# A two-layer GLA and Gated DeltaNet trunk on one core: another order at the program's beginning, a gate product of two matmuls, and stores of the chunk systems in ten pieces

## The reference

```python
def rms_norm(x, w):
    y = xf * lax.rsqrt(jnp.mean(xf * xf, axis=-1, keepdims=True) + NORM_EPS)
    return (y * w.astype(jnp.float32)).astype(x.dtype)

def gdn_mixer(h, w_in, conv_w, a_log, dt_bias, head_norm, w_out):
    proj = h @ w_in
    qkv, z, beta_logit, a_logit = jnp.split(proj, [...], axis=-1)
    ...
    beta = jax.nn.sigmoid(beta_logit.astype(f32))
    log_a = -jnp.exp(a_log.astype(f32)) * jax.nn.softplus(a_logit.astype(f32) + dt_bias.astype(f32))
    ...
    # per head: chunk of 16 meta tokens, then 16 chunks of 64 tokens
    m = jnp.where(strict, jnp.einsum('bhnid,bhnjd->bhnij', kb, k) * decay_mat, 0.0)
    sol = lax.linalg.triangular_solve(m, rhs, left_side=True, lower=True, unit_diagonal=True)
    ...
    o = rms_norm(o, head_norm) * jax.nn.silu(z.astype(f32)).reshape(b, l, GDN_HEADS, GDN_DV)
```

## Time and profile before

| what | us |
|---|---|
| median of 3 runs | 1465.19 (1463.52 to 1466.24) |
| the profiled execution, its own time | 1463.95 |
| its span in the trace | 1462.2 |
| PE busy | 1425.5 |
| DVE busy | 762.5 |
| ACT busy | 461.6 |
| POOL busy | 419.0 |
| mean granted clock of PE | 0.996 of full |

### The profile page before, as it was taken

One profiled execution on the slowest core, in us unless ns is written; L12 is line 12 of the kernel. 1 busy time (PEld: TensorE's weight loads), 2 busy tenths in 40 slices (PEclk: granted clock), 3 DMA queues, 4 the chain that ended last, 5 costly groups with the idle time before them and its releaser, 6 DMA issues.

```text
span 1462.2 us, 21408 instructions
## 1 busy us (share of the span) xinstructions
PE 1425.5 (97%) x8458; PEld 1198.3 (82%) x8458; DVE 762.5 (52%) x937; ACT 461.6 (32%) x957; POOL 419.0 (29%) x358
## 2 busy tenths in 40 slices
PE   7999999999999999999999999999989999999997
PEld 5777799978888888999999999978867767777776
DVE  5223622234444356645645698789944654444442
ACT  4332731133222243333344533421232631111121
POOL 3212043442101121212211167243442441222210
PEclk9999999999999999999999999999999999999999
DMA  5521244476444224444454222336368895555530
GB/s 193 175 87 36 80 131 147 146 254 209 158 159 163 75 58 116 128 107 111 112 155 160 84 80 74 92 92 178 115 210 231 247 233 146 148 148 159 166 87 29
DMA packets 213918, 200.35 MB, mean 137 GB/s; under 512 B 62873, under 2 KB 177065, under 8 KB 213570
## 3 DMA queue, kind: packets, MB, share of 16 engines
q1 hardware_dynamic: 207234, 187.53, 43.0%
q10 hardware_dynamic: 6592, 11.54, 2.9%
HBM read 131.93 MB, written 67.09 MB: 136 GB/s over the span
## 4 chain that ended last, share of the span: by engine, by line
PE 53%; DVE 6%; ACT 2%; DMA 2%; issue 1%; SPq 1%; DVEq 0%; POOLq 0%; ACTq 0%; POOL 0%
PE banks L2157 17%; PE banks L2955 12%; PE banks L2224 12%; DVE gdn L2476 4%; PE banks L2051 2%; PE banks L3044 2%; PE banks L3011 2%; PE banks L3016 2%; PE banks L2075 1%; PE banks L3025 1%; DMA gdn<-gdn_v 1%; PE banks L2999 1%; DMA gdn_z<-gdn 1%; PE banks L2968 1%; ACT gdn L2302 1%
## 5 line engine op out<-in xcount | busy, mean ns | idle before, releaser
L2157 PE MATMUL banks<-hn_hi,gdn 128*128 128x352 f32 x1488 | 300.5, 327 | 0.0
L2157 PEld LDWEIGHTS banks<-hn_hi,gdn 128*128 128x128 f32 x1488 | 242.1, 188 | 4.8 <-issue 3.1
L2476 DVE SCALAR_TENSOR_TENSOR gdn<-gdn,conv_taps,gdn 128x1040 f32<-128x1040 f32 x96 | 175.9, 1832 | 13.6 <-ACT gdn L2288 10.8
L882 PE MATMUL banks<-gdn,hn_hi 128*128 128x512 f32 x528 | 168.1, 400 | 4.0 <-POOL gdn L604 3.1
L2224 PE MATMUL banks<-gdn,hn_hi 128*128 128x512 f32 x512 | 163.8, 400 | 1.8 <-ACT gdn L2423 1.4
L2428 POOL TENSOR_TENSOR gdn<-gdn,gdn 128x1024 fp32r<-128x1024 f32 x31 | 87.1, 2810 | 270.3 <-ACT gdn L2263 270.3
L2157 PE MATMUL banks<-hn_lo,gdn 128*128 128x352 f32 x744 | 158.2, 321 | 0.0
L2157 PEld LDWEIGHTS banks<-hn_lo,gdn 128*128 128x128 f32 x744 | 125.6, 188 | 0.0
L882 PEld LDWEIGHTS banks<-gdn,hn_hi 128*128 128x128 f32 x528 | 99.2, 190 | 28.8 <-ACT gdn L434 3.9
L2224 PEld LDWEIGHTS banks<-gdn,hn_hi 128*128 128x128 f32 x512 | 96.2, 190 | 29.1 <-issue 3.1
L882 PE MATMUL banks<-gdn,hn_lo 128*128 128x512 f32 x264 | 104.5, 396 | 0.0
(11 more groups left out here) (315 smaller groups left out, 2286.4 us busy)
## 6 DMA issues: line engine op xcount, KB each, us to landing
gdn<-in_gdn_w_in SPq DMA_DIRECT2D x32, 512.0 KB, 4.1
gdn<-in_x SPq DMA_DIRECT2D x16, 512.0 KB, 4.1
gdn<-in_gla_w_in SPq DMA_DIRECT2D x32, 256.0 KB, 4.7
gdn_kq<-gdn SPq DMA_DIRECT2D x16, 512.0 KB, 3.8
gdn_v<-gdn SPq DMA_DIRECT2D x16, 512.0 KB, 3.5
gdn<-in_gdn_w_in SPq DMA_DIRECT2D x32, 256.0 KB, 4.8
gdn<-gdn_kq SPq DMA_DIRECT2D x16, 512.0 KB, 3.7
gdn<-gdn_ek SPq DMA_DIRECT2D x16, 512.0 KB, 5.8
```

Of the source, the lines that this page charges most:

```text
L882: mm = pe.matmul(out_bank(g, u, i), h_[:, kt, k], piece_of(w_, q), start=(kt == 0 and e == 0), stop=(kt == KT - 1 and e == 2))
L2157: last = pe.matmul(a[:, b, 0:m], w[n % 2][:, kt, :], x[:, kt, PAD + s:PAD + s + m], start=(kt == 0 and e == 0), stop=(kt == KT - 1 and e = ...
L2476: dve.scalar_tensor_tensor(cv[:, :], xs[:, tap:tap + L], T.cw[:, tap, t:t + 1], cv[:, :], ALU.mult, ALU.add).then_inc(S("ni_conv"), 1)
```

## The change

Four parts.

1. **Beginning.** ACT squares tile 1 before it splits any weights, splits piece 1 sooner, takes the high half of tile 0 before it copies the norm weights, and squares tile 3 ahead of pieces 5 to 7. DVE scales tile 1 from the banks, right behind tile 0; the low half of piece 1 comes ahead of tile 0's, and tile 2 is scaled ahead of the low half of piece 7. POOL takes the roots of tiles 2 and 3 between its low halves.
2. **Gate.** High and low half of the gate weights lie side by side, high at columns 0 to 39 and low at 64 to 103. The high half of the data meets all 104 columns in one matmul, its low half the first 40 in another: two matmuls where there were three. Rows 64 to 103 of the sum then have to be added to rows 0 to 39: ACT copies them out (`gate_low`, three pieces), DVE adds (`gate_logs`, three pieces of 40 rows), and what follows works on whole rows of 1040. PE's wait before tile 3 is for the three adds.
3. **Stores.** The meta systems are weighed ahead of the last part of the inversion (`weigh_meta`), and stored and loaded back at once. Behind `weigh`, SP stores chunk 0 of all heads (8 rows), chunk 1 of all heads (8 rows), issues the meta chunk's loads of v and k, then stores chunks 2 to 15 of each head (eight stores of 14 rows), and loads what chunks 0 and 1 need. The loads of k for them, and ACT's squares of chunk 0, wait for all stores.
4. **Layout.** `og`, one `h` and `kt` move into the space of `sc` that was held by `St` before, and `vn`, `St`, `ua` and the other `h` above it.

Core of the diff:

```diff
             squares(0)
+            squares(1)
             split(0)
-            squares(1)
-            act.wait_ge(S("ai_hn"), 1)
+            split(1)
+            high(0)
+            act.wait_ge(S("ai_hn"), 2)
...
-            for q in range(0, KT, 2):
-                split_lo(q)
+            split_lo(0)
+            split_lo(2)
             rsqrt(2)
+            split_lo(4)
             rsqrt(3)
+            split_lo(6)
...
-                w = nw if t else banks[:, 2:4, :].rearrange("p a n -> p (a n)")
+                w = nw if t > 1 else banks[:, 2:4, :].rearrange("p a n -> p (a n)")
...
+        if n:
+            c = GL + GW if e == 0 else GW
+            return pe.matmul(H.bank[:, 3 * n + b, :][0:c, 0:m], g_w[:, kt, 0:c], x[:, kt, PAD + s:PAD + s + m],
+                             start=(kt == 0 and e == 0), stop=(kt == KT - 1 and e == 1), skip_group_check=True)
...
+            def gate_low():
+                act.wait_ge(S("ni_mm"), GATE + 1)
+                for b, (s, m) in enumerate(SPANS):
+                    act.activation(gate[:, s:s + m], acc[1][GL:GL + GW, b, 0:m], ACT.Copy).then_inc(S("ni_ebeta"), 1)
...
-            sp.wait_ge(S("ni_u"), 4)
+            sp.wait_ge(S("ni_u"), 1)
             sp.dma_start(T.gdn_uam, m_rows).then_inc(S("ni_uam_out"), 16)
-            sp.dma_start(T.gdn_ua, sc[:, 0:2 * C * C].rearrange("p (j x) -> p j x", x=2 * C)).then_inc(S("ni_ua_out"), 16)
+            sp.wait_ge(S("ni_uam_out"), 16)
+            meta_ahead(sp)
+            sp.wait_ge(S("ni_u"), 3)
+            for c in range(2):
+                sp.dma_start(T.gdn_ua.rearrange("(g c) j x -> c g (j x)", c=NCH)[c], sc[c::NCH, 0:2 * C * C])                  .then_inc(S("ni_uam_out"), 16)
+
+        def store_ua(sp):
+            for h in range(NH):
+                rows = slice(h * NCH + 2, (h + 1) * NCH)
+                sp.dma_start(T.gdn_ua[rows], sc[rows, 0:2 * C * C].rearrange("p (j x) -> p j x", x=2 * C))                  .then_inc(S("ni_ua_out"), 16)
...
-            sp.wait_ge(S("ni_uam_out"), 16)
             load_meta()
+            F.store_ua(sp)
+            F.ua_first(sp)
+            load_ua(0)
+            load_ek(1)
+            F.ua_stored(sp)
             load_kt(0)
             load_kt(1)
-            sp.wait_ge(S("ni_ua_out"), 16)
-            load_ua(0)
-            load_ek(1)
...
+                if m == 0:
+                    F.ua_stored(act)
```

118 lines of the change are left out of this document (66 added, 52 removed).

## The result

The changed kernel takes 1480.88 us (median of 4 runs, 1476.12 to 1483.60), beside 1464.36 for the kernel before (4 runs, 1461.34 to 1466.24): 1.0111 times as long, 95% interval 1.0076 to 1.0147. 1462.6 was forecast, with a range up to 1467.0. The profiled execution took 1478.58, 14.6 more than that of before. PE is busy for 1425.1 us, against 1425.5: nearly all of the difference is time in which PE stands still.

The account below looks back on a forecast made before the run. PE, busy for 97% of the span, was taken as the bound, with about 37 us of holes. Beginning -1.5, gate -1.1 and scan 0 summed to -2.6: 1462.6 us as a median, 8-in-10 range 1456.0 to 1467.0.

Parts of the forecast that it names:

- What bounds the kernel: Whole span: PE busy 97%, about 37 us of holes; only shortening PE's work or closing a hole helps.
- the 0.2% (2.9 us): Whole kernel: gain below which measurement can't tell it from no change; the forecast was put within 0.1 us of it.
- Beginning: Program's start: earlier square and scale of tile 1 close PE's holes at the transposes, -1.5 us, bounds 0 and -3.0.
- Gate: Gate's products: 16 fewer matmuls before the barrier save 2.5 us, later gate arithmetic costs 1.4; net -1.1, bounds -2.5 and +0.5.
- Scan: Last scan's beginning: first holes (1.4 us) close, the third grows by as much; 0, bounds -7.3 and +5.9.
- the line 1079.5 + 8 x 1.23: Scan's stores: eight stores' large packets, one round of 1.23 us each, the last at 1089.4.
- the bunched packets: Rival at the scan's stores: busiest engines carry 10 large packets instead of 8, L2976 2.5 us later, 1465.1; chance 0.15.
- the slower rival: Scan: all z stores behind late large packets, L2976 at 1100.0, +5.9, total 1468.5; chance 0.13.
- The rule weighed: Scan's stores: engines used are the largest number up to 16 dividing the slowest dimension; by it 1465.1 would be likeliest.
- Issue time of SP, 0.6 us: SP's queue at the scan: 0.6 us per issue, so the eight stores go from 1078.3 to 1083.
- Where it would show: Signs at beginning, gate and scan: there, large packets in bursts of 8 and 14; bursts ending after 1091 mean the slower side.

Follow-up runs that it names:

- only_start: The kernel before with the change's first part alone (order of squares, splits, roots and scales at the beginning): 1463.33 us, 0.9998 of before.
- only_gate: The kernel before with the change's second part alone (two gate products instead of three, and the adds): 1464.33 us, 1.0005 of before.
- stride9: The changed kernel with nine stores of 14 rows standing nine apart and one of the last two rows: 1468.70 us, 1.0037 of before.
- one_store: The changed kernel with its ten stores made one of 128 rows, ahead of the meta chunk's loads: 1462.64 us, 0.9990 of before.
- eight_near: The changed kernel with sixteen stores of 8 rows standing four apart, within 32 rows, in place of its ten: 1471.73 us (1 run).
- before_split: The kernel before with its one store of 128 rows split into the ten stores, in the same place: 1479.57 us, 1.0108 of before.
- eight_far: The changed kernel with sixteen stores of 8 rows standing sixteen apart in place of its ten: 1491.27 us (1 run).

## Why the prediction was wrong, by its own steps

- **What bounds the kernel**: right, and the holes were the right ones to look at. The forecast's 2.6 us are 0.3 short of the 0.2% (2.9 us) and not 0.1, which changes no chance.
- **Beginning, -1.5 (0 to -3.0)**: right. The square of tile 1 started at 6.67 (6.9 said), the unit ended at 23.0 (22.9 said), and the lead of PE at the barrier beyond the gate's 2.5 was 2.0. In the median of only_start 0.4 is left, within its interval of nothing.
- **Gate, -1.1 (-2.5 to +0.5)**: right term by term, wrong in sum. 16 matmuls fewer were worth 2.5, POOL's low half took the place of the 8 behind the barrier (a wait of 1.26), and the wait for the silu is 3.54 where 3.2 was said. That makes -0.8. Not foreseen: that the clock falls behind a hole of this length, 1.6 us more in this trace, so +0.8, outside the bounds. The forecast charged the wait and put its effect on the clock at nothing. only_gate's median is 0.6 above that of before, within its interval of nothing.
- **Scan, 0 (-7.3 to +5.9)**: here it failed, and the failed step is the price of a round of large packets, 1.23 us, in the line 1079.5 + 8 x 1.23. Every case that times the stores, the bunched packets and the slower rival too, kept this figure for stores of 8 and 14 rows, and worked with how many packets an engine has and when they are issued. 1.24 is what the rows of a 128-row store take. In stores of 14 neighbouring rows they took 2.55 in the mean and up to 5.35, the eight stores needed 30 us instead of 10, and the z stores issued beside them landed after 12 to 22 us. From a lead of 1.4 at 578.86 to 14.6 late at the end the rest of the kernel lost 16.0 us, where +5.9 was the bound. The slower rival had the right place and sign (late z landings hold up L3023) and the wrong reason for the size: it kept the last needed landing 7.3 us behind the last large packet, while here it came at 1104.24, 7 us ahead of the last one's end, and L3023 started at 1104.97 and not at 1100.0. The fall of the clock behind it was foreseen, and costs no more than before (0.82 and 0.79 over 16 us).
- **The rule weighed** was the number of engines. It is the smaller part: stride9, with ten stores and nearly full packet speed, is 6.1 us above one_store, and eight_near, with eight packets at a time, 7.6 above before. The map of rows to ports, on the page of the Trainium skill named above, was the rule that speaks against this change, and it was not looked for.
- **Issue time of SP, 0.6 us**: wrong for the same reason. It is 0.6 while the engines keep up and 2.56 when they don't, so the queue's issue time here follows the packets. It did become a cost: in before_split, eight_far and eight_near PE's longest wait is for a load that SP could not issue sooner. The loads of v ahead of the eight stores took 4.65 us for two, where 0.6 each was the forecast and 1.2 each the slower rival's.
- **Where it would show**: the large packets start in groups of 8 (1074.8), 8 (1077.2) and 14 (1081.9), as said, and a burst pattern that ends after 1091 was named as the sign of the slower side; it ended at 1111.5.

## To carry to other kernels

A store of part of the partitions is not a part of the cost of the whole: which rows go together decides more than how many. One store of all 128 rows, four of 32 rows four apart and four of all rows cut along the free dimension were alike within the spread here; ten stores of 14 rows nine apart cost 6 us more, and neighbouring rows 18. Before splitting a transfer, reckon its packets longer by the number of its rows that share a way (two: 2.2 to 2.5 us, four: about 5, where one takes 1.24), and look at who else has transfers in flight: here another queue's 256 KB stores went from 8 to 10 us to between 12 and 22. A hole that PE shows once was moved but not closed by reordering while a 4 MB transfer of 11 us had to pass in the same stretch; it came back at z, at the meta chunk or at the first two full chunks in every order tried. And look at the clock behind a hole that a change makes longer: the gate's cost 1.6 to 2.8 us there besides its own length, in 11 of the 17 traces that have it.
